# The norm between the two blocks: rwkv's transposes taken from X before it is rewritten

## What is computed

```python
h = rmsnorm(h, final_norm)                 # end of the first block; h is kept as the residual
...
hn = _rms_norm(h, e_norm_mix[0])           # second block, layer 0
p = hn @ e_w_in[0]
pu, pv, pb = _split(p, [A_WIDTH, A_WIDTH, B_IN])
...
h = h + concatenate([ya, yb]) @ e_w_out[0]

def _rms_norm(x, g):
    y = x * rsqrt(mean(x * x, axis=-1) + eps)
    return y * g
```

## Time and profile before

| | |
|---|---|
| median of 3 runs | 2033.1 us (2032.88 to 2034.56) |
| the profiled execution's own time | 2032.94 us |
| its span (first to last instruction) | 2031.0 us |
| PE busy, share of the span | 98% |
| DVE, ACT, POOL busy | 76%, 57%, 20% |
| mean granted TensorE clock | 0.993 of full |

### The profile page before, as it was taken

One profiled execution on the slowest core, in us unless ns is written; L12 is line 12 of the kernel. 1 busy time (PEld: TensorE's weight loads), 2 busy tenths in 40 slices (PEclk: granted clock), 3 DMA queues, 4 the chain that ended last, 5 costly groups with the idle time before them and its releaser, 6 DMA issues.

```text
span 2031.0 us, 31723 instructions
## 1 busy us (share of the span) xinstructions
PE 1981.4 (98%) x11697; PEld 1747.0 (86%) x11697; DVE 1551.4 (76%) x2173; ACT 1152.6 (57%) x1707; POOL 396.9 (20%) x192
## 2 busy tenths in 40 slices
PE   8999998999999999999999999999999999999997
PEld 6888998888888899988889898888998788888885
DVE  6777886777777778677778767777786798888886
ACT  5445664544554455654456535444566677777775
POOL 2222032322222310233222341322002000000000
PEclk9999999999999999999999999999999999999998
DMA  9555531555565544455544004555553688888895
GB/s 354 188 190 191 171 110 63 187 193 193 173 192 195 192 167 156 146 187 186 187 168 164 1 1 167 197 191 192 186 207 116 238 315 324 320 328 325 327 333 183
DMA packets 73395, 401.21 MB, mean 198 GB/s; under 512 B 8256, under 2 KB 8384, under 8 KB 41152
## 3 DMA queue, kind: packets, MB, share of 16 engines
q1 hardware_dynamic: 72848, 398.07, 56.3%
q10 hardware_dynamic: 432, 1.57, 0.2%
HBM read 398.57 MB, written 1.05 MB: 197 GB/s over the span
## 4 chain that ended last, share of the span: by engine, by line
PE 86%; DVE 8%; PEld 3%; ACT 2%; issue 1%; DMA 0%; SPq 0%; ACTq 0%; DVEq 0%; PEldq 0%
PE psum L777 20%; PE psum L315 15%; PE psum L316 14%; PE psum L317 14%; PE psum L757 10%; PE psum L1011 2%; DVE w_lo L290 2%; PE psum L999 2%; PE psum L3102 1%; PEld psum L315 1%; PEld psum L317 1%; PEld psum L316 1%; PE psum L329 1%; DVE w_lo L296 1%; PE psum L2358 1%
## 5 line engine op out<-in xcount | busy, mean ns | idle before, releaser
L290 DVE TENSOR_TENSOR w_lo<-ring,w_hi 128x1024 fp32r<-128x1024 f32 x498 | 739.7, 1515 | 175.2 <-ACT w_hi L283 173.9
L283 ACT ACTIVATE w_hi<-ring 128x1024 fp32r<-128x1024 f32 x744 | 739.9, 1051 | 206.1 <-PEq L509 106.2
L296 POOL TENSOR_TENSOR w_lo<-ring,w_hi 128x1024 fp32r<-128x1024 f32 x132 | 326.0, 2470 | 1098.0 <-ACT w_hi L283 1098.0
L777 PE MATMUL psum<-fT,w_hi 128*128 128x512 f32 x1760 | 421.9, 391 | 3.8 <-ACT w_hi L283 3.8
L777 PEld LDWEIGHTS psum<-fT,w_hi 128*128 128x128 f32 x1760 | 330.3, 189 | 72.0 <-ACT w_hi L283 4.2
L315 PE MATMUL psum<-w_hi,hT_hi 128*128 128x384 f32 (+4 forms) x896 | 321.1, 358 | 4.4 <-DVE hT_lo L1325 2.0
L317 PE MATMUL psum<-w_hi,hT_lo 128*128 128x384 f32 (+4 forms) x896 | 310.3, 346 | 0.0
L316 PE MATMUL psum<-w_lo,hT_hi 128*128 128x384 f32 (+4 forms) x896 | 310.0, 346 | 0.0
L315 PE MATMUL psum<-w_hi,act_hi 128*128 128x512 f32 x596 | 234.5, 393 | 0.8 <-DVE act_lo L3382 0.7
L757 PEld LDWEIGHTS psum<-fT,w_lo 128*128 128x128 f32 x1760 | 226.0, 191 | 8.9
L316 PE MATMUL psum<-w_lo,act_hi 128*128 128x512 f32 x596 | 233.5, 392 | 0.0
(11 more groups left out here) (507 smaller groups left out, 2384.2 us busy)
## 6 DMA issues: line engine op xcount, KB each, us to landing
ring<-in_stream SPq DMA_DIRECT2D x249, 1024.0 KB, 5.4
ring<-in_stream SPq DMA_DIRECT2D x248, 512.0 KB, 4.3
tables<-in_tables SPq DMA_DIRECT2D x1, 2261.0 KB, 19.8
gain_row<-in_gains ACTq DMA_DIRECT2D x3, 512.0 KB, 3.7
rows<-in_rows SPq DMA_DIRECT2D x1, 1288.0 KB, 22.7
X<-in_x SPq DMA_DIRECT2D x1, 1024.0 KB, 4.9
result<-X SPq DMA_DIRECT2D x2, 512.0 KB, 3.3
columns<-in_columns SPq DMA_DIRECT2D x1, 993.0 KB, 15.0
```

The lines of the kernel that those rows point to most:

```text
L283: act.activation(part(w_hi, g, i), ring[:, k, i * PART:(i + 1) * PART], ACT.Copy) \
L290: dve.tensor_tensor(part(w_lo, g, i), ring[:, k, i * PART:(i + 1) * PART], part(w_hi, g, i).bitcast(F32), ALU.subtract) \
L296: pool.tensor_tensor(part(w_lo, g, 2), ring[:, k, 2 * PART:STEP], part(w_hi, g, 2).bitcast(F32), ALU.subtract) \
L777: pe.matmul(psum[:, 4 + 2 * (s % 2) + o, :], w[0][:, o, k, :], fT[:, k, :, :].rearrange("p a c -> p (a c)"), start=k == 0, stop=False, ski ...
```

## The change

The final norm gives h = x r1 g1 with r1 = 1/rms(x), and rwkv's norm gives h r2 g2. The token factors r1 r2 can be kept apart from the channel factors g1 g2. So the transposes take X before the rewrite. `joint_gain`, the product of both weights as columns, is made once by DVE when the delta stage begins, from the ten norms' weight columns, to which final_norm is added as an eleventh group. The evictions scale by it. `final_vector` puts 1/rms into rstd_f and waits for the last transpose before it rewrites X. rwkv's statistics are taken from the rewritten X as before; `stats_vector` multiplies rstd by rstd_f, with one more product and wait, ahead of the diagonals, and "norm 7 rstd" now stands for the product. On PE `head_tensor` for rwkv is called by `ffn_tensor` right after the last down projection, and the sixteen warming matmuls are gone. On ACT `head_scalar` for rwkv comes between `load_gain_row` and `norm_scalar`, on DVE `head_vector` comes ahead of `final_vector`.

```diff
+        joint_gain = sb("joint_gain", [P, KT])
...
         def rstd_vector(dve, n, t):
-            dve.reciprocal(rstd[:, t:t + 1], rms[:, t:t + 1]).then_inc(*norm.vector())
+            dve.reciprocal(rstd_f[:, t:t + 1], rms[:, t:t + 1]).then_inc(*norm.vector())
...
+        def after_final(n):
+            return n > 0 and NETWORK[n - 1][0] == "final"
...
         def gain_of(n):
+            if after_final(n):
+                return joint_gain
...
         def head_tensor(pe, n, pairs=PAIRS):
-                        pe.wait_ge(*after(f"x {n} {t} {k}"))
+                        pe.wait_ge(*after(f"x {n - after_final(n)} {t} {k}"))
...
         def head_scalar(act, n, pairs=PAIRS):
                 act.wait_ge(*after(f"norm {n} turn {p}"))
+                if after_final(n):
+                    act.wait_ge(*after("joint gain"))
...
         def stats_vector(dve, n, factor=None):
             dve.reciprocal(rstd[:, :], rms[:, :]).then_inc(*norm.vector(f"norm {n} rstd"))
             dve.wait_ge(*norm.vector.so_far())
+            if after_final(n):
+                dve.tensor_tensor(rstd[:, :], rstd[:, :], rstd_f[:, :], ALU.mult).then_inc(*norm.vector(f"norm {n} rstd"))
+                dve.wait_ge(*norm.vector.so_far())
...
             down(n - 1, n - 1, False, True)
-            if NETWORK[at + 1][0] != "final":
-                head_tensor(pe, at + 1)
+            head_tensor(pe, at + 1 + (NETWORK[at + 1][0] == "final"))
...
         def final_vector(dve, at):
             for t in range(TT):
                 rstd_vector(dve, at, t)
-            for t, ins in enumerate(gained(dve, at, X)):
+            dve.wait_ge(*after(f"norm {at + 1} turn {PAIRS[-1]}"))
+            for t, ins in enumerate(gained(dve, at, X, rstd_f)):
...
-                elif NETWORK[at - 1][0] == "final":
-                    keep_warm(pe, psum[:, 7, :], 16)
-                    head_tensor(pe, at)
...
                         load_gain_row(act, n)
+                        head_scalar(act, at + 1)
                         norm_scalar(act, at)
                 elif kind != "moe":
-                    head_scalar(act, at, (3,) if after_mixer(at) else PAIRS)
+                    if not after_final(at):
+                        head_scalar(act, at, (3,) if after_mixer(at) else PAIRS)
...
                 if at == first_mixer:
                     dve.wait_ge(loaded, 16 * LOADS)
+                    dve.tensor_tensor(joint_gain[:, :], col("gain")[:, KT * 6:KT * 7], col("gain")[:, KT * 10:KT * 11], ALU.mult) \
+                       .then_inc(*norm.vector("joint gain"))
                 if kind == "final":
                     if NETWORK[at - 1][0] != "moe":
+                        head_vector(dve, at + 1)
                         final_vector(dve, at)
                     continue
                 if kind != "moe":
-                    head_vector(dve, at, (3,) if after_mixer(at) else PAIRS)
+                    if not after_final(at):
+                        head_vector(dve, at, (3,) if after_mixer(at) else PAIRS)
```

More of the change, by code:

```diff
@@ L68, in __getitem__ @@
         return slice(*self.at[name])
-COLUMN = Places([("gain", 10 * KT), ("conv", 4 * 12), ("mu", 14), ("w0", 4), ("a0", 4), ("k_k", 4), ("k_a", 4),
+COLUMN = Places([("gain", 11 * KT), ("conv", 4 * 12), ("mu", 14), ("w0", 4), ("a0", 4), ("k_k", 4), ("k_a", 4),
                  ("r_k", 4), ("sgu_b", 4), ("sgu_w", 4 * P), ("router", KT * EXPERTS), ("lora", 512), ("g2", 512),
@@ L901, in load_gain_row, with gained @@
             act.dma_start(gain_row[:, :], gains_in[which].partition_broadcast(P)).then_inc(row_loaded, 16)
-        def gained(dve, at, to):
+        def gained(dve, at, to, scale=rstd):
             dve.wait_ge(row_loaded, 16 * sum(kind in ("final", "moe") for kind, _ in NETWORK[:at + 1]))
             for t in range(TT):
-                yield dve.scalar_tensor_tensor(to[:, t, :], X[:, t, :], rstd[:, t:t + 1], gain_row[:, :], ALU.mult, ALU.mult)
+                yield dve.scalar_tensor_tensor(to[:, t, :], X[:, t, :], scale[:, t:t + 1], gain_row[:, :], ALU.mult, ALU.mult)
         def final_vector(dve, at):
@@ L3666, in pack_columns @@
     names = ["l0_ffn1_norm", "l0_mix_norm", "l0_ffn2_norm", "l1_ffn1_norm", "l1_mix_norm", "l1_ffn2_norm",
-             "e_norm_mix_2", "e_norm_ffn_2", "o_norm_mix_2", "o_norm_ffn_2"]
+             "e_norm_mix_2", "e_norm_ffn_2", "o_norm_mix_2", "o_norm_ffn_2", "final_norm"]
     c[:, COLUMN["gain"]] = np.concatenate([per(a[n].reshape(-1)) for n in names], axis=1)
```

## The result

The changed kernel takes 2036.94 us (median of 15 runs, 2035.71 to 2039.16) against 2032.98 for the kernel before (15 runs, 2029.54 to 2035.69): a ratio of 1.0021, 95% interval 1.0015 to 1.0028. It is **4 us slower** where 2.3 us of gain were forecast. The profiled execution took 2035.80 us with a span of 2033.8, which is 1.1 under that median. Against the profiled execution before (2032.94, span 2031.0) it lost 2.9 us, so two executions show a little less than the runs do.

A forecast was written before the change was run, and what follows sets the result against it. PE bounds the kernel, holding 86% of the chain that ended last. The first projection comes 7.64 us earlier, a 3.9 us wait leaves 3.6, clock loss 1.3 leaves 2.3: 2033.1 becomes 2030.8 us, range 2029.0 to 2032.6.

The forecast's parts named there:

- The first projection: First matmul of the rwkv projections, after the final norm: claimed to move from 1048.63 to 1040.99.
- 7.64 us: How much earlier the first rwkv projection was to start; the whole gain if nothing else held PE.
- The wall: Ahead of rwkv's row matmul after step 0: PE waits 3.9 us for the diagonal, row at 1053.3, only 3.6 earlier.
- The rival without a wall: At the row matmul: diagonal ready by 1050 or downstream slack won; gain over 4.1 up to 7.64 us, chance 0.10.
- The table load: Sqrt load on ACT after the evictions: warm activation 1.30 us after its start; rival with a 1.3 us stall, chance 0.02.
- POOL's split: Last third of rwkv's step 1 split, 1053.81 to 1056.20; limits the gain at the sixteenth matmul to 2.85 us.
- The clock: At the wait before the row matmul: granted clock falls to 0.50, loss 0.75 to 1.7 us, taken as 1.3.
- Carried to the end unchanged: After rwkv's first steps: later queues have slack, so the 2.3 us gain lasts to the kernel's end.
- Edits at nothing: Small edits, among them joint gain and eight more columns in the first load, priced at no cost; joint gain uncovered 0.1 to 0.2.
- The rival on the slower side: In rwkv's steps 1 and 2: clock stays at 1.2 GHz, loss 5.1 us, 2034.6; chance 0.05.

The follow-up runs named there:

- layout alone: The kernel before, in its old order, with the wider column table, the added joint_gain tile and its one product: 2040.76 us, ratio 1.0037.
- pads: The kernel before with two unused tiles of 32 bytes per partition where the added columns and joint_gain stand: 2039.01 us, ratio 1.0030.
- w by 64: The kernel before with one unused tile of 64 bytes directly ahead of w_hi: 2038.93 us, ratio 1.0025.
- the order alone: The changed kernel with the kernel before's memory: final norm's weight loaded into gain_row, product taken in place; 2029.94 us, ratio 0.9988 to the kernel before.
- the changed kernel with the old distance: The changed kernel with squares and rms declared ahead of hT_hi, hT_hi to w_hi again 63552 bytes: 2029.52 us, ratio 0.9985 to the kernel before.
- warmed kernel: The order alone plus fifteen unawaited warming matmuls on PE in the wait ahead of the row matmul: 2026.71 us, ratio 0.9973.

## Why the prediction was wrong

The first steps stood, and one that was costed at nothing decided the result.

- **The first projection**, forecast at 1040.99: 1041.08. About 1.0 of the 7.64 us was a low stretch at 1045.2 that not every execution has: in the three kernels with the old order and no fall there (layout alone, pads, w by 64) the first projection comes 10.3 us after the first update of X, not 11.32. **The wall**, row matmul forecast at 1053.3: 1053.35, released by the diagonal, with the table load, the roots, the rewrite and the split of step 1 in the order of the working. The wait was 3.31 us where 3.9 stood, since PE's step 0 ended at 1050.04: its 72 matmuls took 8.68 us from the first start to the last, 8.14 before and 8.43 with the order alone. The rival without a wall fell.
- **The table load** took what the rows of delta said: load at 1042.61, next activation at 1043.91, 1.30 later. The Trainium skill (ScalarE: Activation LUTs, "What ACT_TABLE_LOAD costs") would add a drain of about 1380 ns; nothing of it stands between these rows, nor ahead of the load, which starts when the evictions end (1039.57 + 3.03).
- **POOL's split** was forecast for 1053.81 and started at 1053.94. The gain behind it without a clock loss was forecast at 2.85, and in the run of the changed kernel with the old distance, where the clock didn't fall, it is 3.08 (66.82 - 63.74). That kernel does wait for POOL at the sixteenth matmul, 0.61 us.
- **The clock** was mis-sized a little, and this is the smaller error. It fell for 3.4 us on resumption, the late end of the range, a loss of 1.7 where 1.3 was taken. The changed kernel keeps 66.82 - 65.36 = 1.46 at the spread matmuls where 2.3 was forecast. From the row matmul to there it takes 49.54 us against 47.24: 1.7 of these 2.3 are the clock, and 0.5 the layout, which works in this stage too.
- **Carried to the end unchanged**: right for the order of work. The order alone gives 2029.94 and the changed kernel at the old distance 2029.52, with ratios of 0.9988 and 0.9985 (2.4 and 3.0 us), both in the range and near the forecast's 2.3. Part of this is luck. In the profiled execution of the order alone nothing of the gain is left at the end of rwkv (195.59 us from the first update of X to the first by rwkv's output, 195.42 before), for the clock fell twice in it; its last rewrite still comes 3.0 us earlier, because a fall of 6.8 us near 1578 is missing. With the old distance and no fall in rwkv the stage takes 192.36, which is 3.06 kept to its end.
- **The step that failed** stands under "Edits at nothing": "Eight more columns in the first load: some bytes in a transfer." The bytes are indeed nothing. But the wider table and the tile of the joint gain both lie between hT and w in memory, and 64 bytes of distance cost 2.2 us in the sparse stage, 2.4 in the experts, 1.0 in delta, 0.7 in attention, and 6 by the medians of the kernel with nothing but pads. I had read the edit as traffic and as an instruction, never as a layout.
- **The rival on the slower side** had the right sign and the wrong cause. It laid a loss on a clock that stays low through steps 1 and 2; the clock was low for 3.4 us there (6.8 in the order alone). None of the rivals had the place of a tile in it, so the range's upper end of 2032.6 had no room for it.

Two of the measured sizes can be added up: by medians the order gives -3.0, the pads +6.1, together +3.1, against +4.0 measured. The rest is within the spread of such differences, in which low stretches of the clock play.

## What to carry to other kernels

An edit that adds or widens a tile moves every tile declared behind it, so price it as a change of layout too. Look at the mean duration, and at the start to start distance, of the longest matmul groups in stages that the edit doesn't touch, and try an unused pad before blaming or praising the order of work. A wait that PE gets from being earlier is priced by what releases it, here statistics behind a rewrite and a split; moving the waiting matmul behind more ready work gave 4.0 us by the medians, and filling the wait with warming matmuls 3.2. The second number is that of a clock that no longer falls: the row came no sooner.

## What was not expected of the hardware

- **A matmul's pace depends on where its two operands lie.** With hT_hi and w_hi 63552 bytes apart a 128x256 matmul of the sparse stage takes 276 to 279 ns, with 63616 or 63488 it takes 282 to 285 (with 63680 about 279, and 1.3 us for the stage), in the same instruction stream with no wait. At 63584, 63616 and 63680 the expert stage is 2.1 to 3.6 us longer as well, but not at 63488.
- **Falls of the clock aren't certain.** A wait of 3.57 us at the row matmul left the clock at 1.00 in the changed kernel with the old distance, 3.31 us brought it down for 3.4 us in the changed kernel, and 3.56 us for 6.8 us in the order alone. The stretches about that wall in the first one (columns as above):

```profile
1049.50:1052.90 3.40, 0.00 (x0) 0.00 (x0) 3.29 (x7) 1.69 (x4) 0.00 (x0) 1.00 0.00 0
1052.90:1056.30 3.40, 2.77 (x22) 2.58 (x23) 1.51 (x4) 0.68 (x2) 2.39 (x1) 1.00 0.84 292
```

- **The falls lie at a handful of places and come in steps.** Near 13, 327, 349, 1050, 1104, 1134 and 1580 us each profiled execution has some of them (further ones after 2005 us aside), and each lasted 3.4 or 6.8 us. The 12 runs of the order alone cluster about 2026.4, 2029.8 and 2034.0, and the mean granted clock of each run goes with it: 0.996 in the three fastest, 0.993 or 0.994 in the five about 2029.8, 0.992 in the four slowest. 0.004 of 2030 us is 8.1 us, near the 7.6 between the outer clusters, as falls would cost that halve the pace. Where they lay in each run isn't known, since one execution of each kernel was profiled. Of the warmed kernel's 7 runs six lie between 2026.3 and 2026.8, where the order alone has its fastest cluster.
